# Seven-product pairs at every fourth expert instead of every sixth, with the low parts of their rows made by accumulating transfers

## The chip, the cores and the metric

One core of one Trainium2 chip. The metric is the device time of one launch in microseconds (us); lower is better.

## The reference, cut to what matters

Two transformer blocks run one after the other on 256 tokens of width 1024. The change touches only the last stage, the mixture of experts at the end of the second block:

```
def chunk_fn(args):
    xt, et, gt = args
    act = jax.nn.gelu(jnp.einsum('td,tkd->tk', xt, u_tab[et])) * gt
    return jnp.einsum('tk,tkd->td', act, v_tab[et])
```

There are 128 x 128 experts. Each token picks 128 of them (8 heads with 16 each). The kernel doesn't gather: it computes a dense product of all experts with all tokens, in which the share of an expert that a token didn't pick is zero. The last product is then out[token, d] = sum over all experts of key[expert, token] times v_tab[expert, d], where key is the gated activation.

## The kernel before, in words

**Blocks of experts.** The kernel calls 128 experts with one first index "expert e". Its keys are the 128 x 256 slice `gates_all[:, e, :]` (128 experts by 256 tokens), and its row is a 128 x 1024 piece of v_tab that SP's queue streams from HBM into one of six slots of `ring` (`chunk_done` of the chunk six places earlier frees the slot). The change is in the stage that goes over e = 0 to 125 and adds into PSUM banks. This stage is the last large one; a short tail for two more experts, the final norm and the store follow it.

**Parts.** Each float32 factor is split into a high part, rounded to the format that TensorE multiplies, and the rest, the low part. A product is then three matmuls: high by high, high by low, low by high. ACT makes the high part of a row (`hi`, L747) and of keys (`key_high`, L1147). The low part is a subtraction, whole minus high. DVE makes it for these rows (`lo`, L1369) and keys (`key_low`, L2030); GpSimd (POOL) does so in earlier stages and is idle in this one. There are three places for high rows and three for keys, used in turn.

**One expert, `second(e)`.** Two halves of the tokens by two halves of the width are four products of 128x128 by 128x512, so twelve matmuls (L2781 to L2783).

**A pair, `seven(e)`.** Two experts e and e+1 together are a product of 2x2 blocks, which would be eight block products. The Winograd form of Strassen's method does it with seven, 21 matmuls instead of 24 (L2853 to L2855), from sums and differences of the blocks. The extra work beside the matmuls: four key sums of 128x128 (`sums_of_keys`, L2051 to L2056), four row sums of 128x512 (`first_sum_of_rows`, `sums_of_rows`, L2073 to L2083), and the high and low parts of all these sums (`key_sums_high` and `row_sums_high` on ACT, `key_sums_low` L2060 and `row_sums_low` L2087 on DVE). Of the row of e only the first half is used as it is (`half_of`), of e+1 the whole row. Pairs start at e = 18 and then at every sixth e, 18 pairs in all; the four experts between two pairs use `second`.

**Order.** Each engine has its own list of instructions, written by hand, and semaphores between them. `chunk_done` counts the chunks that TensorE has finished. Within a pair it is raised after the fourth product (the chunk of e is done) and after the seventh (the chunk of e+1 is done). The place of the row sums is reused as that of their low parts, so DVE may begin the sums for the next pair only when the pair before is finished. The same held for the key sums: they lay where their low parts go.

Of the kernel before, what the change touches and what calls it, by code (L numbers as in the profile page):

```python
# [17 lines left out]
P = 128  # L18
# [30 lines left out]
SEVEN_FROM, SEVEN_TO = 18, NA  # L49
# [28 lines left out]

def _split_plan():
# [5 lines left out]
    for name, n in STAGES:  # L85
        for r in range(n):
# [14 lines left out]
            if who:  # L101
                made["hi"] += (name, r) not in OWN
                made[who] += 1
# [6 lines left out]
            lo.append(made[who] if who else None)  # L110
# [37 lines left out]
def build(nc, x_d, meta_d, pos_d, stream_d, cols_d, w1_d, w2_d, w3_d, zt_d, decay_d, dft_d, idft_d, mask_d, sq_d, keys_d, out_d):  # L148
    with ExitStack() as ctx:
# [50 lines left out]
        keys_split = over("keys_split", "aux", NW * CW + 6 * T, [P, 2, 4, P])  # L200
        sums_lo, sums_hi = over("sums_lo", "arena", 0, [P, 4, 512]), over("sums_hi", "arena", 4 * 512, [P, 4, 512])
# [113 lines left out]
        def vt(n):  # L315
# [26 lines left out]
        key_sums = aux[:, NW * CW + 6 * T + 4 * P:NW * CW + 6 * T + 8 * P].rearrange("p (a t) -> p a t", a=4)  # L342
        row_sums = arena[:, 0:4 * 512].rearrange("p (a d) -> p a d", a=4)
# [13 lines left out]
        lo_pool, lo_dve, own_hi = sem("lo_pool"), sem("lo_dve"), sem("own_hi")  # L357
# [18 lines left out]
        loaded_part = [sem(f"loaded_part{n}") for n in range(KT // 2)]  # L376
        flt_pe, flt_arg, flt_sin, flt_k = sem("flt_pe"), sem("flt_arg"), sem("flt_sin"), sem("flt_k")
# [15 lines left out]
        vt_turned, vt_ready, spec_ready, ys_ready = sem("vt_turned"), sem("vt_ready"), sem("spec_ready"), sem("ys_ready")  # L393
# [6 lines left out]
        cv_ready, ce_ready, ew_ready, ew_turned, halves_added = (  # L400
            sem("cv_ready"), sem("ce_ready"), sem("ew_ready"), sem("ew_turned"), sem("halves_added"))
# [3 lines left out]
        xt_turned, xt_ready, xt_added = sem("xt_turned"), sem("xt_ready"), sem("xt_added")  # L405
# [84 lines left out]
        N_SEVEN = (SEVEN_TO - SEVEN_FROM) // 6 - 1  # L490

        def row_of(e, i):

            if i is None:
                return gates_all[:, e, :]
            return gates_all[:, bass.ds(i * 6 + e, 1), :].rearrange("p a t -> p (a t)")
# [5 lines left out]
        def sevens(e):  # L502

            return (e - SEVEN_FROM) // 6
# [116 lines left out]
        def _(pool):  # L621
# [48 lines left out]
            for n, c in enumerate(OWN_CHUNKS):  # L670
# [3 lines left out]
                nc.gpsimd.tensor_copy(hi_part(c), ring[:, c % NS, :]).then_inc(own_hi, 1)  # L674
                if BY[c] == "pool":
                    pool.wait_ge(own_hi, n + 1)
# [17 lines left out]
            lo(base + NA)  # L694
            lo(base + expert_u(NA))
# [3 lines left out]
        def _(act_e):  # L699
# [444 lines left out]
            def key_high(e, i=None, w=T):  # L1144

                act_e.wait_ge(chunk_done, turns(base + NA + e - 2, i, 6))
                A(peer_part[0][:, e % 3, 0:w], row_of(e, i)[:, 0:w], ACT.Copy).then_inc(key_hi, 1)  # L1147

            def key_and_row(e, i=None):

                key_high(e, i)
                hi(base + expert_v(e), 0 if i is None else i, 6 if i is not None else 0)

            def half_of(e, i=None):
# [3 lines left out]
                act_e.wait_ge(landed[c % NS], turns(16 * (c // NS + 1), i, 16))  # L1158
                act_e.wait_ge(chunk_done, turns(BEFORE[c] + 1, i, 6))
                A(hi_part(c)[:, 0:512], ring[:, c % NS, 0:512], ACT.Copy).then_inc(hi_ready, 1)  # L1160

            def key_sums_high(e, i=None):

                act_e.wait_ge(sums_made, turns(8 * sevens(e) + 4, i, 8))
                A(keys_split[:, 0, :, :], key_sums, ACT.Copy).then_inc(sums_hi_ready, 1)

            def row_sums_high(e, half, i=None):

                act_e.wait_ge(sums_made, turns(8 * sevens(e) + 6 + 2 * half, i, 8))
# [8 lines left out]

            for e in range(NW, SEVEN_FROM):
                hi(base + expert_v(e))  # L1180
            key_sums_high(SEVEN_FROM)
            seven_ahead(SEVEN_FROM)
            with act_e.Fori(0, N_SEVEN) as i:
                for m in range(2, 6):
                    key_and_row(SEVEN_FROM + m, i)
                key_sums_high(SEVEN_FROM + 6, i)
                seven_ahead(SEVEN_FROM + 6, i)
            for e in range(SEVEN_TO - 4, NA):
                key_and_row(e)
                if e in (SEVEN_TO - 2, SEVEN_TO - 1):  # L1190
# [1871 lines left out]
```

## Time and profile before

| what | value |
|---|---|
| median of 3 runs | 1702.54 us (1701.95 to 1702.57) |
| the profiled execution | 1702.42 us, of which the trace's span is 1700.6 us |
| TensorE busy | 1684.0 us (99%) |
| VectorE (DVE) busy | 1315.4 us (77%) |
| ScalarE (ACT) busy | 1010.1 us (59%) |
| GpSimd (POOL) busy | 817.2 us (48%), nothing between about 1341 and 1675 us |
| data moved | 296.38 MB, mean 174 GB/s |

The profiled time is 1.8 us longer than the span: start and end lie outside the trace. Matmuls overlap in the trace (each is shown some 390 ns long, though they follow each other more closely), so a busy TensorE doesn't tell how fast it goes; the distance between two starts does. The stage of the change fills most of the time between 1370 and 1680 us.

### The profile page before, as it was taken

What the parts mean: (1) busy time and instruction counts of PE and PEld (TensorE: products, weight loads), DVE (VectorE), ACT (ScalarE), POOL (GpSimd) and SP (SyncE); (2) the same over time, 40 slices, a digit from 0 to 9 for tenths busy, and PEclk for the clock granted to TensorE, in tenths of its full rate; (3) what the DMA queues carried; (4) which work ended last, traced back from release to release, by engine and by line L of the source; (5) the groups of instructions that cost most, each with busy time, mean ns of one, the idle gap of its engine ahead of it and who ended that gap; (6) DMA issues with size and microseconds to landing.
All of it is one profiled execution on the core that took longest, in us unless ns stands there. A gap on an engine that the chain in (4) does not pass through costs nothing.

```text
span 1700.6 us, 33402 instructions
## 1 busy us (share of the span) xinstructions
PE 1684.0 (99%) x11335; PEld 1528.8 (90%) x11335; DVE 1315.4 (77%) x2539; ACT 1010.1 (59%) x1701; POOL 817.2 (48%) x341
## 2 busy tenths in 40 slices
PE   9999999999999999999999999999999999999998
PEld 8988898889998888988999999999999988888887
DVE  6767786566547777869877998777888779999997
ACT  5444632566564445657555555887878546666665
POOL 4666596842766666742006782777777400000001
PEclk9999999999999999999999999999999999999999
DMA  7655454622445554443555455444444555555553
GB/s 252 210 185 190 160 188 148 211 100 100 149 160 187 185 188 171 161 160 127 173 186 186 171 186 178 172 163 162 164 168 165 173 194 194 198 201 193 199 199 116
DMA packets 85841, 296.38 MB, mean 174 GB/s; under 512 B 10548, under 2 KB 14613, under 8 KB 85606
## 3 DMA queue, kind: packets, MB, share of 16 engines
q1 hardware_dynamic: 82480, 290.69, 49.9%
q10 hardware_dynamic: 3254, 4.23, 0.8%
q8 instruction: 72, 1.18, 0.3%
q14 instruction: 35, 0.29, 0.1%
HBM read 293.83 MB, written 1.05 MB: 173 GB/s over the span
## 4 chain that ended last, share of the span: by engine, by line
PE 92%; DVE 5%; ACT 1%; DMA 0%; issue 0%; SPq 0%; POOL 0%; DVEq 0%; POOLq 0%; ACTq 0%
PE ps L2223 15%; PE ps L2225 15%; PE ps L2224 14%; PE ps L2329 6%; PE ps L2781 5%; PE ps L2782 5%; PE ps L2783 5%; PE ps L2330 3%; PE ps L2356 2%; PE ps L2357 2%; PE ps L2478 2%; PE ps L2358 2%; PE ps L2825 2%; PE ps L2853 2%; PE ps L2854 2%; PE ps L2855 2%
## 5 line engine op out<-in xcount | busy, mean ns | idle before, releaser
L2225 PE MATMUL ps<-h_lo_hi,ring_lo 128*128 128x256 f32 (+1 forms) x1888 | 531.5, 282 | 0.0
L627 POOL TENSOR_TENSOR ring_lo<-ring,peer_split 128x1024 fp32r<-128x1024 f32 x117 | 283.7, 2425 | 451.2 <-ACT peer_split L747 448.7
L627 POOL TENSOR_TENSOR ring_lo<-ring,main_hi 128x1024 fp32r<-128x1024 f32 x114 | 285.5, 2505 | 182.6 <-ACT main_hi L747 161.2
L2225 PEld LDWEIGHTS ps<-h_lo_hi,ring_lo 128*128 128x128 f32 x1888 | 355.8, 188 | 0.0
L627 POOL TENSOR_TENSOR ring_lo<-ring,more_hi 128x1024 fp32r<-128x1024 f32 x89 | 229.0, 2573 | 188.6 <-ACT more_hi L747 182.9
L2223 PE MATMUL ps<-h_lo_hi,peer_split 128*128 128x256 f32 x1024 | 288.1, 281 | 0.1
L2224 PE MATMUL ps<-h_lo_hi,peer_split 128*128 128x256 f32 x1024 | 286.8, 280 | 0.0
L747 ACT ACTIVATE peer_split<-ring 128x1024 fp32r<-128x1024 f32 x238 | 249.4, 1048 | 29.4 <-PE ps L2783 29.4
L747 ACT ACTIVATE main_hi<-ring 128x1024 fp32r<-128x1024 f32 x156 | 164.3, 1057 | 96.6 <-DMA ring<-in_stream 72.8
L2224 PEld LDWEIGHTS ps<-h_lo_hi,peer_split 128*128 128x128 f32 x1024 | 193.8, 189 | 0.0
L2223 PEld LDWEIGHTS ps<-h_lo_hi,peer_split 128*128 128x128 f32 x1024 | 193.2, 189 | 0.3 <-issue 0.2
L1369 DVE TENSOR_TENSOR ring_lo<-ring,peer_split 128x1024 fp32r<-128x1024 f32 x121 | 148.8, 1230 | 38.6 <-ACT peer_split L747 38.3
L747 ACT ACTIVATE more_hi<-ring 128x1024 fp32r<-128x1024 f32 x111 | 117.6, 1061 | 92.4 <-DMA ring<-in_stream 82.0
L2223 PE MATMUL ps<-h_lo_hi,main_hi 128*128 128x256 f32 (+1 forms) x504 | 145.1, 288 | 1.5 <-DVE ring_lo L1369 1.1
L2781 PE MATMUL ps<-peer_split 128*128 128x512 f32 x368 | 146.0, 397 | 0.0
L2782 PE MATMUL ps<-ring_lo,peer_split 128*128 128x512 f32 x368 | 144.5, 393 | 0.0
L2783 PE MATMUL ps<-peer_split 128*128 128x512 f32 x368 | 143.6, 390 | 0.0
L2224 PE MATMUL ps<-h_lo_hi,main_hi 128*128 128x256 f32 (+1 forms) x504 | 141.8, 281 | 0.0
L2330 PE MATMUL ps<-h_lo_hi,ring_lo 128*128 128x256 f32 x448 | 125.3, 280 | 0.0
L1147 ACT ACTIVATE peer_split<-arena 128x256 fp32r (+3 forms) x108 | 43.0, 398 | 106.4 <-PE ps L2783 75.4
L2223 PEld LDWEIGHTS ps<-h_lo_hi,main_hi 128*128 128x128 f32 x504 | 95.2, 189 | 8.5 <-issue 6.1
L2224 PEld LDWEIGHTS ps<-h_lo_hi,main_hi 128*128 128x128 f32 x504 | 95.2, 189 | 0.5 <-issue 0.2
(552 smaller groups left out, 4299.9 us busy)
## 6 DMA issues: line engine op xcount, KB each, us to landing
ring<-in_stream SPq DMA_DIRECT2D x550, 512.0 KB, 3.2
x<-in_x SPq DMA_DIRECT2D x4, 256.0 KB, 5.1
arena<-in_decay ACTq DMA_DIRECT2D x4, 256.0 KB
arena<-in_keys ACTq DMA_DIRECT2D x1, 1024.0 KB, 5.5
out<-h SPq DMA_DIRECT2D x7, 128.0 KB, 2.0
arena<-in_mask ACTq DMA_DIRECT2D x1, 768.0 KB, 5.4
aux<-in_dft ACTq DMA_DIRECT2D x4, 72.0 KB
arena<-in_filter_w ACTq DMA_DIRECT2D x1, 260.0 KB
```

The source lines that it names most:

```text
L627: nc.gpsimd.tensor_tensor(ring_lo[:, c % NS, :], ring[:, c % NS, :], hi_part(c).bitcast(F32), ALU.subtract).then_inc(lo_pool, 1)
L747: A(hi_part(c), ring[:, c % NS, :], ACT.Copy).then_inc(hi_ready, 1)
L1147: A(peer_part[0][:, e % 3, 0:w], row_of(e, i)[:, 0:w], ACT.Copy).then_inc(key_hi, 1)
L1369: V.tensor_tensor(ring_lo[:, c % NS, :], ring[:, c % NS, :], hi_part(c).bitcast(F32), ALU.subtract).then_inc(lo_dve, 1)
L2223: M(out, w_hi, parts[0], start=start, stop=False, skip_group_check=True)
L2224: M(out, w_hi, parts[1], start=False, stop=False, skip_group_check=True)
L2225: return M(out, w_lo, parts[0], start=False, stop=stop, skip_group_check=True)
L2329: M(out, hi_part(c)[:, cols_at], h_lo_hi[:, :, k, NM:L], start=(k == 0), stop=False, skip_group_check=True)
L2330: ins = M(out[:, 1, :], ring_lo[:, c % NS, cols_at], h_lo_hi[:, 1, k, NM:L], start=False, stop=(k == KT - 1), skip_group_check=True)
L2781: M(by_token(t, b), a_hi, w_hi, start=begin, stop=False)
L2782: M(by_token(t, b), a_hi, w_lo, start=False, stop=False)
L2783: return M(by_token(t, b), a_lo, w_hi, start=False, stop=end)
```

## The change

From e = 30 on a pair starts at every fourth e, so that two experts by `second` follow each pair. The pairs at 18 and 24 stay as they were, and the ones at 30, 34, ... 122 are new in form: 24 pairs in place of the 16 that stood at 30, 36, ... 120. In these the low parts of the two rows no longer come from DVE. ACT writes the negated high part of the row into a new place `pair_low` (`minus_high`: 128x512 of the row of e, 128x1024 of the row of e+1), and a DMA issued by GpSimd adds the whole row onto it, which leaves whole minus high. TensorE waits for these transfers by two new semaphores, `low_moved[0]` and `low_moved[1]`. ACT still makes the high parts as before. `pair_low` exists once, so ACT may write it only when the chunk of the first expert of the pair before is done. The key sums of these pairs lie in a place of their own (`late_key_sums`), so that DVE can make them while TensorE still uses the parts of the pair before; their high part waits on ACT for the end of that pair. Both new places lie on keys that are used up by then. The loops go over twelve experts at a time instead of six. Three semaphores of earlier stages are merged into one, `side_turned`.

```
 def minus_high(e, i=None):
+    for n, (c, at, width) in enumerate(((base + expert_v(e), 0, 512), (base + expert_v(e + 1), 512, CW))):
+        if n == 0:
+            act_e.wait_ge(chunk_done, turns(base + expert_v(e - 4) + 1, i, GROUP))
+        act_e.wait_ge(landed[c % NS], turns(16 * (c // NS + 1), i, 16 * GROUP // NS))
+        A(pair_low[:, at:at + width], ring[:, c % NS, 0:width], ACT.Copy, scale=-1.0).then_inc(other_hi, 1)
...
 # ACT, for each pair
+def four_behind(e, i=None):
+    key_and_row(e + 2, i)
+    key_and_row(e + 3, i)
+    minus_high(e + 4, i)
+    key_sums_high(e + 4, i)
+    seven_ahead(e + 4, i)
...
 # GpSimd
+for e in range(FOUR_FROM, NA, 4):
+    for n, (c, at, width) in enumerate(((base + expert_v(e), 0, 512), (base + expert_v(e + 1), 512, CW))):
+        pool.wait_ge(other_hi, len(OWN) + 2 * (sevens(e) - 2) + n + 1)
+        pool.dma_start(pair_low[:, at:at + width].bitcast(F32), ring[:, c % NS, 0:width], accum_op=ALU.add).then_inc(low_moved[n], 16)
...
 # DVE, for each pair
+def four_behind(e, i=None):
+    row_sums_low(e, 1, i)
+    row_and_key(e + 2, i)
+    sums_of_keys(e + 4, i)
+    row_and_key(e + 3, i)
+    pair_ahead(e + 4, i)
+
+def pair_ahead(e, i=None):
+    dve.wait_ge(chunk_done, turns(base + expert_v(e - 2), i, GROUP))
     first_sum_of_rows(e, i)
-    half_of(e, i)
     sums_of_rows(e, i)
     key_low(e + 1, i)
+    key_sums_low(e, i)
     dve.wait_ge(sums_made, made(8, e, i))
-    lo(base + expert_v(e + 1), 0 if i is None else i, 6 if i is not None else 0, 6 if i is not None else 0)
     row_sums_low(e, 0, i)
...
 # TensorE
+def both_parts(n, c):
+    if by_dma(e):
+        pe.wait_ge(hi_ready, turns(HI[c], i, GROUP))
+        pe.wait_ge(low_moved[n], turns(16 * (sevens(e) - 1), i, 16 * GROUP // 4))
+    else:
+        low(c)
...
+with pe.Fori(0, N_GROUPS) as i:
+    for m in range(0, GROUP, 4):
+        seven(FOUR_FROM + m, i=i)
+        second(FOUR_FROM + m + 2, i=i, step=GROUP, los=GROUP // 2)
+        second(FOUR_FROM + m + 3, i=i, step=GROUP, los=GROUP // 2)
```

On ACT the loop over the experts stood like this at the step from the single experts to the next pair (L1147 copies keys, L747 a whole row, L1165 the key sums, L1160 half of a row):

```order
L1147 ACTIVATE peer_split<-arena 128x256
L747 ACTIVATE peer_split<-ring 128x1024 [waits chunk_done,landed5]
L1164 ISA
L1165 ACTIVATE keys_split<-aux 128x512 [waits sums_made]
L1146 REGISTER_ALU
L1147 ISA [waits chunk_done]
L1147 ACTIVATE peer_split<-arena 128x128
L1158 REGISTER_ALU
L1160 ACTIVATE peer_split<-ring 128x512 [waits chunk_done,landed0]
```

The same place of the changed kernel (L1167 copies keys, L767 a whole row, L1207 the negated rows, L1187 the key sums, L1180 half of a row):

```order
L1167 ACTIVATE peer_split<-arena 128x256
L767 ACTIVATE peer_split<-ring 128x1024 [waits chunk_done,landed3]
L1207 ACTIVATE pair_low<-ring 128x512 [waits landed4,chunk_done]
L1207 ACTIVATE pair_low<-ring 128x1024 [waits landed5]
L1185 REGISTER_ALU
L1186 ISA [waits chunk_done]
L1187 ACTIVATE keys_split<-arena 128x512 [waits sums_made]
L1163 ISA [waits chunk_done]
L1167 ACTIVATE peer_split<-arena 128x128
L1180 ACTIVATE peer_split<-ring 128x512 [waits chunk_done,landed4]
```

Two copies have come between the last single row and the key sums, and the key sums wait for `chunk_done` too.

On GpSimd nothing stood between the last rows of the stage before and the end of the program:

```order
L626 REGISTER_ALU [waits lo_pool]
L627 TENSOR_TENSOR ring_lo<-ring,peer_split 128x1024 [waits hi_ready]
L632 REGISTER_ALU
L632 COMPARE_AND_BRANCH
L627 TENSOR_TENSOR ring_lo<-ring,peer_split 128x1024 [waits hi_ready,lo_pool] x3
L149 UNCONDITIONAL_BRANCH
```

In the changed kernel 24 times two transfers stand there, of which the first and the last two are shown:

```order
L643 TENSOR_TENSOR ring_lo<-ring,peer_split 128x1024 [waits hi_ready,lo_pool]
L714 DMA pair_low<-ring 128x512 [waits other_hi]
L714 DMA pair_low<-ring 128x1024 [waits other_hi]
...
L714 DMA pair_low<-ring 128x512 [waits other_hi]
L714 DMA pair_low<-ring 128x1024 [waits other_hi]
L643 TENSOR_TENSOR ring_lo<-ring,peer_split 128x1024 [waits hi_ready,lo_pool] x2
L158 UNCONDITIONAL_BRANCH
```

Each transfer waits for one copy of ACT, and nothing else of GpSimd stands between them.

On DVE the work ahead of a pair held two low parts of rows (L2041 and L1369) among the sums of rows (L2080 to L2083) and the keys (L2030):

```order
L2041 TENSOR_TENSOR ring_lo<-ring,peer_split 128x512 [waits sums_made,hi_ready]
L2080 TENSOR_TENSOR arena<-ring,arena 128x512 [waits sums_made,landed1]
L2081 TENSOR_TENSOR arena<-ring 128x512
L2082 REGISTER_ALU
L2083 TENSOR_TENSOR arena<-ring,arena 128x512 [waits sums_made]
L2029 REGISTER_ALU
L2030 TENSOR_TENSOR peer_split<-arena,peer_split 128x256 [waits key_hi]
L2095 REGISTER_ALU
L1368 REGISTER_ALU
L1369 TENSOR_TENSOR ring_lo<-ring,peer_split 128x1024 [waits hi_ready]
```

In the changed kernel they are gone, and the low part of the key sums (L2107) comes after the sums of rows (L2127 to L2132) instead of ahead of them:

```order
L2127 TENSOR_TENSOR arena<-ring,arena 128x512 [waits sums_made]
L2073 REGISTER_ALU
L2074 TENSOR_TENSOR peer_split<-arena,peer_split 128x128 [waits key_hi]
L2130 TENSOR_TENSOR arena<-ring 128x512
L2131 REGISTER_ALU
L2132 TENSOR_TENSOR arena<-ring,arena 128x512 [waits sums_made]
L2073 REGISTER_ALU
L2074 TENSOR_TENSOR peer_split<-arena,peer_split 128x256 [waits key_hi]
L2106 REGISTER_ALU
L2107 TENSOR_TENSOR keys_split<-arena,keys_split 128x512 [waits sums_hi_ready]
```

What stays is one subtraction for keys between the sums of rows, and DVE reads no row's high part for a pair any more.

## Rows read from the trace of the kernel before

**Rows 1.** The page: busy time of each engine, and the chain that ended last.
```profile
PE 1684.0 (99%) x11335; PEld 1528.8 (90%) x11335; DVE 1315.4 (77%) x2539; ACT 1010.1 (59%) x1701; POOL 817.2 (48%) x341
...
PE 92%; DVE 5%; ACT 1%; DMA 0%; issue 0%; SPq 0%; POOL 0%; DVEq 0%; POOLq 0%; ACTq 0%
```

**Rows 2.** Busy time by stretch, 1420 to 1500 us (columns in the first line).
```profile
core 0: us, PE busy (x) PEld busy (x) DVE busy (x) ACT busy (x) POOL busy (x), PEclk, DMA share, GB/s
1420.00:1500.00 80.00, 80.00 (x348) 64.97 (x348) 73.41 (x116) 50.23 (x76) 0.00 (x0) 1.00 0.57 197
```

**Rows 3.** Waits from 1360 to 1690 us: engine, line, waited for, total, times, longest.
```profile
POOL ring_lo L627 <- ACT peer_split L747: 335.0, 2, 334.6
ACT peer_split L1147 <- PE ps L2783: 75.4, 54, 1.9
DVE ring_lo L1369 <- ACT peer_split L747: 32.7, 65, 5.9
ACT peer_split L1147 <- PE ps L2855: 31.0, 36, 1.1
```

**Rows 4.** TensorE's timeline (start, duration): a pair's first, twelfth and last matmul, the next pair.
```profile
1504.56 0.40 PE L2853 MATMUL ps<-peer_split 128*128 128x512 f32 x1
...
1507.11 0.39 PE L2855 MATMUL ps<-sums_hi,keys_split 128*128 128x512 f32 x1
...
1509.18 0.39 PE L2855 MATMUL ps<-sums_hi,peer_split 128*128 128x512 f32 x1
...
1520.50 0.40 PE L2853 MATMUL ps<-peer_split 128*128 128x512 f32 x1
```

**Rows 5.** DVE's timeline around the same pair (start, duration).
```profile
1499.42 0.69 DVE L2060 TENSOR_TENSOR keys_split<-aux,keys_split 128x512 fp32r<-128x512 f32 x1
1500.02 0.69 DVE L2073 TENSOR_TENSOR arena<-ring 128x512 f32<-128x512 f32 x1
1500.63 0.29 DVE L2030 TENSOR_TENSOR peer_split<-arena,peer_split 128x128 fp32r<-128x128 f32 x1
1500.83 0.69 DVE L2041 TENSOR_TENSOR ring_lo<-ring,peer_split 128x512 fp32r<-128x512 f32 x1
...
1506.98 1.23 DVE L1369 TENSOR_TENSOR ring_lo<-ring,peer_split 128x1024 fp32r<-128x1024 f32 x1
1508.11 0.42 DVE L2030 TENSOR_TENSOR peer_split<-arena,peer_split 128x256 fp32r<-128x256 f32 x1
...
1512.24 0.42 DVE L2030 TENSOR_TENSOR peer_split<-arena,peer_split 128x256 fp32r<-128x256 f32 x1
1512.58 0.29 DVE L2051 TENSOR_TENSOR aux<-arena 128x128 f32 x1
...
1512.99 0.28 DVE L2054 TENSOR_TENSOR aux<-aux,arena 128x128 f32<-128x128 f32 x1
1513.40 0.29 DVE L2056 TENSOR_TENSOR aux<-arena,aux 128x128 f32<-128x128 f32 x1
```

**Rows 6.** ACT's timeline around the same pair (start, duration).
```profile
1503.36 2.00 ACT L1170 ACTIVATE sums_hi<-arena 128x1024 fp32r<-128x1024 f32 x2
...
1507.64 0.42 ACT L1147 ACTIVATE peer_split<-arena 128x256 fp32r x1 [1.02 <-PE ps L2855]
1507.96 1.04 ACT L747 ACTIVATE peer_split<-ring 128x1024 fp32r<-128x1024 f32 x1
...
1513.75 0.61 ACT L1165 ACTIVATE keys_split<-aux 128x512 fp32r<-128x512 f32 x1
1515.25 0.31 ACT L1147 ACTIVATE peer_split<-arena 128x128 fp32r x1 [0.89 <-PE ps L2783]
1515.46 0.62 ACT L1160 ACTIVATE peer_split<-ring 128x512 fp32r<-128x512 f32 x1
```

**Rows 7.** DMA from 1500 to 1532 us: packets, MB, share; issues, KB each, us to landing.
```profile
q1 hardware_dynamic: 1728, 6.29, 57.0%
...
ring<-in_stream SPq DMA_DIRECT2D x12, 512.0 KB, 3.2
```

More of the change, by code:

```diff
@@ L76, with by_dma @@
 OUT1_SLOT = (1, 2, 0, 4, 5, 0, 1, 2)
+def by_dma(e):
+    return e >= FOUR_FROM and (e - FOUR_FROM) % 4 < 2
 def _split_plan():
@@ L100, in _split_plan @@
                 who = "dve"
-            if who:
+            if name == "experts" and NA <= r < 2 * NA and by_dma(r - NA):
+                who = "dma"
+                made["hi"] += 1
+            elif who:
                 made["hi"] += (name, r) not in OWN
@@ L109, in _split_plan @@
             hi.append(made["hi"])
-            lo.append(made[who] if who else None)
+            lo.append(made[who] if who in made else None)
             same = [b for b in range(c) if by[b] and slot[b] == slot[c] and (b >= START["experts"]) == (name == "experts")]
@@ L502, in sevens, with sums_of_pair @@
         def sevens(e):
-            return (e - SEVEN_FROM) // 6
+            return (e - SEVEN_FROM) // 6 if e < FOUR_FROM else 2 + (e - FOUR_FROM) // 4
+        def sums_of_pair(e):
+            return late_key_sums if by_dma(e) else key_sums
         LEAD, AFTER = 3, 2
@@ L1151, in key_and_row @@
                 key_high(e, i)
-                hi(base + expert_v(e), 0 if i is None else i, 6 if i is not None else 0)
+                hi(base + expert_v(e), 0 if i is None else i, GROUP if i is not None else 0)
             def half_of(e, i=None):
@@ L2048, in sums_of_keys @@
                 a11, a21, a12, a22 = a0[:, 0:P], a0[:, P:T], a1[:, 0:P], a1[:, P:T]
[L2049 to L2050 removed]
+                s1, s2, s3, s4 = (sums_of_pair(e)[:, n, :] for n in range(4))
+                if by_dma(e):
+                    dve.wait_ge(sums_lo_ready, turns(3 * sevens(e) - 2, i, 9))
+                else:
+                    dve.wait_ge(chunk_done, base + expert_v(e - 4))
                 V.tensor_tensor(s1, a21, a22, ALU.add).then_inc(sums_made, 1)
@@ L2109, in _ @@
             seven_ahead(SEVEN_FROM)
-            with dve.Fori(0, N_SEVEN) as i:
-                row_sums_low(SEVEN_FROM, 1, i)
+            for e in range(SEVEN_FROM, FOUR_FROM, 6):
+                row_sums_low(e, 1)
                 for m in range(2, 5):
-                    row_and_key(SEVEN_FROM + m, i)
-                sums_of_keys(SEVEN_FROM + 6, i)
-                row_and_key(SEVEN_FROM + 5, i)
-                seven_ahead(SEVEN_FROM + 6, i)
-            row_sums_low(SEVEN_TO - 6, 1)
-            for e in range(SEVEN_TO - 4, NA):
-                row_and_key(e)
+                    row_and_key(e + m)
+                sums_of_keys(e + 6)
+                row_and_key(e + 5)
+                if e + 6 < FOUR_FROM:
+                    seven_ahead(e + 6)
+            pair_ahead(FOUR_FROM)
+            with dve.Fori(0, N_GROUPS) as i:
+                for m in range(0, GROUP, 4):
+                    four_behind(FOUR_FROM + m, i)
+            for e in range(FOUR_FROM + N_GROUPS * GROUP, NA - 4, 4):
+                four_behind(e)
+            row_sums_low(NA - 4, 1)
+            row_and_key(NA - 2)
+            row_and_key(NA - 1)
             def expert(tile, n, buf, part):
@@ L2877, in _ @@
                     second(m, i=i, step=6)
-            seven(SEVEN_FROM, begin=True)
-            for m in range(2, 6):
-                second(SEVEN_FROM + m)
-            with pe.Fori(0, N_SEVEN - 1) as i:
-                seven(SEVEN_FROM + 6, i=i)
-                for m in range(8, 12):
-                    second(SEVEN_FROM + m, i=i, step=6)
-            seven(SEVEN_TO - 6, end=True)
-            for e in range(SEVEN_TO - 4, NA):
-                second(e)
+            for e in range(SEVEN_FROM, FOUR_FROM, 6):
+                seven(e, begin=e == SEVEN_FROM)
+                for m in range(2, 6):
+                    second(e + m)
+            with pe.Fori(0, N_GROUPS) as i:
+                for m in range(0, GROUP, 4):
+                    seven(FOUR_FROM + m, i=i)
+                    second(FOUR_FROM + m + 2, i=i, step=GROUP, los=GROUP // 2)
+                    second(FOUR_FROM + m + 3, i=i, step=GROUP, los=GROUP // 2)
+            for e in range(FOUR_FROM + N_GROUPS * GROUP, NA, 4):
+                seven(e, end=e == NA - 4)
+                second(e + 2)
+                second(e + 3)
             pe.wait_ge(sums_kept, 4)
```

137 lines of the change are left out of this document (80 added, 57 removed).

## The prediction

> **What bounds the kernel now.** I read the page's busy times and its chain first [rows 1]: TensorE is busy 99% of the span and holds 92% of the chain that ended last. So a change pays only by giving TensorE less to do, or by ending a wait of TensorE. Next the stage of the change, by stretches [rows 2]: TensorE is busy for all of it at the full granted clock (1.00, which is 2.4 GHz), DVE 73.41 of 80 us, ACT 50.23, POOL not at all, and the DMA engines 0.57 of the time. Then the list of waits there [rows 3]: ACT waits for TensorE, DVE for ACT, and no row says that a matmul waited for anything. POOL's 335.0 us are its pause. TensorE is thus the bound, and its time is the number of matmuls by their spacing.
>
> **The spacing.** A pair starts at 1504.56 and the next at 1520.50 [rows 4]: 15.94 us for 21 + 4 x 12 = 69 matmuls, 0.231 us each, with no gap in between. (The 0.39 to 0.40 us shown for one is its way through a pipeline.)
>
> **What the change removes on TensorE.** From e = 30 there are 24 pairs in place of 16, so 8 more, each with 21 matmuls in place of 24: 24 matmuls by 0.231 are 5.54 us. A group of four experts then takes 21 + 24 = 45 matmuls, 10.40 us. That is all there is to gain, and it holds only while every other engine is done with a group within 10.40 us and every operand is there in time. So I cost each engine per group, counting from start to start in the timeline, since successive instructions of an engine overlap a little.
>
> **DVE, per group.** Four 128x1024 subtractions (two single rows, two halves of the row sums) at 1.13 (1506.98 to 1508.11): 4.52. Five 128x512 ones (four row sums, the key sums' low part) at 0.60 (1499.42 to 1500.02): 3.00. Three key parts at 0.34 (1512.24 to 1512.58): 1.02, and half a key part 0.20 (1500.63 to 1500.83). The four key sums: 1512.58 to the last start at 1513.40 is 0.82, and 0.20 for that one: 1.02. One row sum now needs the one just before it; a dependent start is shown 0.13 after the end of its source (1512.99 + 0.28 to 1513.40), so 0.69 + 0.13 in place of 0.60: 0.22. Sum 9.98 of 10.40 us [rows 5]. The two row parts taken off DVE are 0.60 + 1.13 = 1.73 per pair; with them it would be 11.71, over the limit. So without the transfers the denser pairs could not pay. DVE keeps 0.42 us per group.
>
> **ACT, per group** [rows 6]. Three key copies at 0.32, half of one 0.21, three whole rows at about 0.98, two sums 1.90 together (shown as 2.00), half a row and the key sums some 0.55 each: about 7.1. Added are the negated rows, 128x512 and 128x1024 like the copies there: 0.6 + 1.0. About 8.7 of 10.40: it fits. What matters is where they stand in ACT's list. Queued behind them are the key sums, the half row, the row of e+1 and the row sums of the coming pair, and DVE waits for those. I followed this chain from the start of a pair (0): its twelfth matmul starts 2.55 later, and ACT's key copy 0.53 after that (1507.11 to 1507.64), at 3.1; the row to 4.4; the negated parts end at 5.0 and 5.95; the pair before is over by then (its 21st matmul at 4.6, and 0.5), so the key sums don't wait; half a row to 7.3. The row of e+1 of the coming pair needs the third place of high rows, free after 33 matmuls, 7.6 + 0.5: ACT copies keys and row until 9.5 and row sums to 10.4 and 11.4. DVE finishes the low parts at 11.6 and 12.7. TensorE wants the first with the tenth matmul of the coming pair, 10.40 + 2.08 = 12.5, the second with the sixteenth, 13.9. Spare: 0.9 us at the tightest. I cost these moves at nothing; the cover is this 0.9 us and DVE's 0.42 us.
>
> **The transfers.** POOL has nothing else to do, so it issues each when ACT's copy is done: the 256 KB one at 5.0, the 512 KB one at 5.95. TensorE wants the first at 10.40 and the second three matmuls later, at 11.09. So they may take 5.4 and 5.1 us from issue to landing, and beyond that TensorE stands still in every one of the 23 groups that follow a group of the new form. The trace holds no accumulating transfer, so I bound it. The nearest row is a load of 512 KB: 3.2 us to landing, and twelve of them fill 0.57 of 32 us, so one keeps the 16 engines busy for 1.52 us, and 1.68 us are neither [rows 7]. Floor: 3.2. Two ring loads fall in the same time: the one that replaces the pair's second row (issued at about 5.4) and the one after the next single row (8.1). With an accumulating transfer at the price of a plain one, and all of the 1.68 ahead of the data, data move from 6.7: 0.76 + 1.52, and 1.52 for the first load, end at 10.5; the second load starts to move at 9.8 and shares for 0.7, so 10.5 to 10.9, just inside 11.09. At twice the price (the place is read as well as the source) and with all of both loads ahead of it, 1.52 + 3.04 + 3.04 from 6.7 end at 14.3, 3.2 too late: ceiling 23 x 3.2 = 74 us. I take the plain price, as the nearest row has it, because the 1.68 is not all ahead of the data and the ring load need not win every turn. It is the weakest step of the sum: a delay of 0.24 us per pair eats the whole gain (23 x 0.24 = 5.5).
>
> No row shows what an accumulating transfer costs. The Trainium skill has a rule against it, in *Collectives: The Full Stack*, section "Part 3: Why 7× under link rate — side-by-side accounting": a sum made in the DMA path emits two reads for each write, and such a transfer runs at about half the rate of a copy. By that rule the sum would be that of the first rival below at twice the price, a loss; no run here shows yet whether it holds between two places of SBUF.
>
> **Everything else.** The loads of the ring come as often per matmul as before; the one that must land first, the row of e+1, is issued as a pair starts (0.5), lands at 3.7 and is negated from 5.0 on, 1.3 spare. The unrolled loops and merged semaphores put no work on TensorE. The tail keeps its instructions.
>
> **Sum.** 1702.42 (profiled) less 5.54 is 1696.9; the median of the runs is 0.12 above the profiled one, so 1697.0.
>
> **Rivals.**
> - *The accumulating transfers land late* (the other side). Place: TensorE before the first or fourth matmul of a pair. For it: the window is only 0.2 to 0.6 us wider than a plain price with both ring loads, and an addition must read its place. Against: POOL is free and the DMA engines idle for 0.43 of the time. It decides from a landing of 5.3 us on. At one and a half times the plain price, data end at 6.7 + 1.14 + 2.28 + 1.52 = 11.6 and 12.1 with the second load: 1.05 late, 24 us, so 1721. At twice: 12.8, some 13.6 with the load, 2.5 late, 57 us, so 1754; if half of the 1.68 lies behind or is not there, some 1730. Chance 0.31.
> - *DVE becomes the bound.* It would fill 96% of a group, where it fills 92% now. If each of its 14 instructions cost 0.05 more, 9.98 becomes 10.68, 0.28 over: 23 x 0.28 = 6.4, so 1703. Against it: the prices come from the same instructions in the same stage. Chance 0.09.
> - *Ring loads land late*, because the added 768 KB per pair sit before them. If the row of e+1 is negated 0.6 us later for it, the second transfer lands 0.5 us late: 11.5 less 5.5, so 1708. Chance 0.05.
> - *The change doesn't do what it says*: the matmuls go, but TensorE's time is taken back a little everywhere, 1700 to 1704. Chance 0.03.
>
> **How the numbers follow.** The forecast, no wait of TensorE, has 0.52. Its own range is 1695.8 to 1699.0. A measurement of this kernel can tell about 0.2%, 3.4 us, from no change. Faster by more than that: 0.52. Within it: 0.03 of the late transfers (0.09 to 0.39 us per pair), 0.05 of DVE, 0.01 of the loads and 0.03 of the last rival, 0.12. Slower: the remaining 0.36. The range has to reach into the late transfers: up to 1735 it leaves out some 0.11 above and 0.03 below 1695.8.
>
> **What would show it.** Right: no wait of a matmul on `low_moved`, 45 matmuls in 10.40 us, transfers that land within 5.1 us, DVE at about 0.96. Wrong: a gap before each pair's first or fourth matmul, with the row that follows it released by a DMA; then the price of the accumulating transfers failed. A gap before the tenth or sixteenth would say that ACT's longer list failed, and a gap before a single expert that DVE did.

## The result, and the profile after

The changed kernel took 1804.66 us in the median (1802.60 to 1809.15, 4 runs), beside 1702.24 us for the kernel before on the same chip. The ratio is 1.0605, with a 95% interval of 1.0592 to 1.0618: 102 us slower, where 5.5 us faster was forecast and the range ended at 1735.

The page of the changed kernel, the lines that answer to [rows 1]:

```profile
PE 1722.0 (95%) x11311; PEld 1546.0 (86%) x11311; DVE 1313.8 (73%) x2579; ACT 1056.9 (58%) x1773; POOL 859.4 (48%) x389
...
PE 79%; DMA 9%; DVE 5%; ACT 3%; issue 2%; POOL 1%; SPq 0%; ACTq 0%; DVEq 0%; POOLq 0%
```

TensorE has the 24 matmuls less (11311 for 11335), but is busy longer, and 9% of the chain that ended last are now a DMA. A busy time that grows while the count falls says that something got slower, not only later. The same stretch as [rows 2]:

```profile
1420.00:1500.00 80.00, 64.95 (x235) 49.52 (x234) 51.74 (x90) 43.80 (x67) 8.60 (x10) 0.87 0.69 186
```

235 matmuls instead of 348 in 80 us. TensorE stood still for 15 us of them, DVE fell from 73.41 to 51.74 (so it isn't the bound), and the granted clock is 0.87 of full speed. The waits of the stage, as in [rows 3], below POOL's own pause (316.0 us):

```profile
ACT peer_split L1167 <- PE ps L2937: 99.6, 22, 6.9
DVE ring_lo L1413 <- ACT peer_split L767: 79.6, 34, 5.6
PE ps L2935 <- DMA pair_low<-ring: 46.3, 23, 3.4
PEld ps L2935 <- issue: 34.4, 21, 3.9
PEld ps L2935 <- DVE peer_split L2074: 28.9, 9, 3.6
```

The longest of these rows are followers: DVE waits for ACT, and ACT for TensorE. TensorE waits at one line, L2935, the first matmul of a block product of a pair. PE and PEld (its weight loads) wait at the same time, so their rows must not be added. The row that names DVE is the same wait with another name: TensorE waits there for several things, and a kernel that differs only in the transfer (below, `e1_no_transfer`) has no such row. One pair, to be held against [rows 4]:

```profile
1485.62 0.49 PE L2935 MATMUL ps<-peer_split 128*128 128x512 f32 x1
1485.95 0.40 PE L2936 MATMUL ps<-pair_low,peer_split 128*128 128x512 f32 x1
1486.19 0.40 PE L2937 MATMUL ps<-peer_split 128*128 128x512 f32 x1
1489.33 0.79 PE L2935 MATMUL ps<-peer_split 128*128 128x512 f32 x1 [2.74 <-DMA pair_low<-ring]
1489.91 0.63 PE L2936 MATMUL ps<-pair_low,peer_split 128*128 128x512 f32 x1
1490.34 0.63 PE L2937 MATMUL ps<-peer_split 128*128 128x512 f32 x1
...
1495.04 0.52 PE L2936 MATMUL ps<-sums_lo,keys_split 128*128 128x512 f32 x1
1495.39 0.39 PE L2937 MATMUL ps<-sums_hi,keys_split 128*128 128x512 f32 x1
1495.62 0.40 PE L2935 MATMUL ps<-sums_hi,peer_split 128*128 128x512 f32 x1
...
1501.87 0.40 PE L2935 MATMUL ps<-peer_split 128*128 128x512 f32 x1
```

Three things are to be seen. The fourth matmul, the first that needs the second transfer, stands 2.9 us late (1486.19 to 1489.33, where 0.23 is due). After it, matmuls follow each other at 0.43 us in place of 0.23: TensorE had stood still, and its clock fell to the lower of its two levels (1.2 GHz in place of 2.4) until 1495, which the granted clock of 0.50 in this stretch shows:

```profile
1489.40:1495.00 5.60, 5.60 (x13) 4.38 (x14) 0.54 (x3) 1.33 (x3) 0.00 (x0) 0.50 0.13 37
```

14 steps took 6.06 us where 3.23 were due, another 2.8 us. And the group takes 16.25 us to the next pair, where 10.40 were forecast. The chain of the same pair tells where the transfer's time went:

```profile
1478.95 0.53 ACT pair_low L1207
1479.77 0.86 POOL pair_low L714
1480.72 8.38 DMA pair_low<-ring
1489.33 0.79 PE ps L2935
```

From GpSimd's first issue (1479.77) to the second landing (1489.10) are 9.33 us. DMA from 1478 to 1490 us, as in [rows 7]:

```profile
q1 hardware_dynamic: 573, 2.09, 54.1%
q0 software_dynamic: 288, 0.79, 34.1%
issues: line engine op xcount, KB each, median us to landing
ring<-in_stream SPq DMA_DIRECT2D x3, 512.0 KB, 4.9
pair_low<-ring POOLq DMA_DIRECT2D x1, 512.0 KB, 8.4
pair_low<-ring POOLq DMA_DIRECT2D x1, 256.0 KB, 5.7
```

The pair's 0.79 MB took 34.1% of 12 us, 4.1 us of all 16 engines; the ring's 2.09 MB, 2.6 times as many bytes, took 6.5 us. A byte of an accumulating transfer kept the engines busy 1.7 times as long as one from HBM in this stretch. Within the 9.33 us alone, 1479.77 to 1489.10, the ring's queue (q1) and GpSimd's (q0) filled the engines almost wholly:

```profile
q1 hardware_dynamic: 408, 1.47, 50.2%
q0 software_dynamic: 288, 0.79, 43.9%
```

So the ring's loads took 4.7 us of it, for 1.47 MB or nearly three loads, the pair's own transfers 4.1, and about 0.5 us were neither.

Over all 23 groups, from the starts of the matmuls in the trace: the first pair of the new form starts at 1424.82 and the 24th at 1770.58, 15.03 us per group. The mean of the gap ahead of a pair's first matmul is 0.37 us, ahead of the fourth 2.76, and the steps after it are 1.46 us longer than at full clock, in 16 of the 23 groups by 1.5 us or more and in 7 by 0.1. 23 x (0.37 + 2.76) are 72 us of waiting and 23 x 1.46 are 34 us of the lower clock; less the 5.5 us saved that makes 100 of the 106.7 us by which this span (1807.3 us; the execution shown is the slowest of the four) is longer than the one before (1700.6). In three of the 7 groups without the lower clock the wait ahead of the fourth matmul was 1.8 us or less; in the other four it was 2.7 to 3.2, as long as in the 16.

### The profile page after: what moved, and what is told of

Its sections match the earlier page's. It is cut to its first block, busy times and chain, and to the rows that moved or that the text cites. A ratio compares the mean times of both kernels' runs of the same rounds, so it can differ in the third digit from the quotient of the medians.

```text
span 1807.3 us, 33438 instructions
## 1 busy us (share of the span) xinstructions
PE 1722.0 (95%) x11311; PEld 1546.0 (86%) x11311; DVE 1313.8 (73%) x2579; ACT 1056.9 (58%) x1773; POOL 859.4 (48%) x389
## 4 chain that ended last, share of the span: by engine, by line
PE 79%; DMA 9%; DVE 5%; ACT 3%; issue 2%; POOL 1%; SPq 0%; ACTq 0%; DVEq 0%; POOLq 0%
PE ps L2295 14%; PE ps L2297 14%; PE ps L2296 13%; DMA pair_low<-ring 8%; PE ps L2401 6%; PE ps L2402 3%; PE ps L2935 2%; PE ps L2428 2%; PE ps L2429 2%; PE ps L2550 2%; PE ps L2430 2%; PE ps L2936 2%; PE ps L2937 2%; PE ps L2897 2%; PE ps L2853 2%
## 5 line engine op out<-in xcount | busy, mean ns | idle before, releaser
L767 ACT ACTIVATE peer_split<-ring 128x1024 fp32r<-128x1024 f32 x230 | 240.9, 1048 | 27.1 <-PE ps L2855 27.1
L714 POOL DMA_DIRECT2D pair_low<-ring x48 | 41.5, 865 | 384.5 <-ACT pair_low L1207 382.4
L767 ACT ACTIVATE main_hi<-ring 128x1024 fp32r<-128x1024 f32 x156 | 164.5, 1057 | 95.4 <-DMA ring<-in_stream 70.6
L1413 DVE TENSOR_TENSOR ring_lo<-ring,peer_split 128x1024 fp32r<-128x1024 f32 x89 | 110.7, 1244 | 117.3 <-ACT peer_split L767 117.0
L767 ACT ACTIVATE more_hi<-ring 128x1024 fp32r<-128x1024 f32 x111 | 117.5, 1061 | 85.2 <-DMA ring<-in_stream 79.2
L1167 ACT ACTIVATE peer_split<-arena 128x256 fp32r (+3 forms) x108 | 41.5, 384 | 167.3 <-PE ps L2937 134.1
L2853 PE MATMUL ps<-peer_split 128*128 128x512 f32 x304 | 120.5, 396 | 0.6 <-DVE peer_split L2200 0.6
L2854 PE MATMUL ps<-ring_lo,peer_split 128*128 128x512 f32 x304 | 119.4, 393 | 0.0
L2855 PE MATMUL ps<-peer_split 128*128 128x512 f32 x304 | 118.8, 391 | 0.0
L2295 PEld LDWEIGHTS ps<-h_lo_hi,main_hi 128*128 128x128 f32 x504 | 95.2, 189 | 8.5 <-issue 6.1
```

The lines of the kernel that those rows point to most:

```text
L714: pool.dma_start(pair_low[:, at:at + width].bitcast(F32), ring[:, c % NS, 0:width], accum_op=ALU.add).then_inc(low_moved[n], 16)
L767: A(hi_part(c), ring[:, c % NS, :], ACT.Copy).then_inc(hi_ready, 1)
L1413: V.tensor_tensor(ring_lo[:, c % NS, :], ring[:, c % NS, :], hi_part(c).bitcast(F32), ALU.subtract).then_inc(lo_dve, 1)
L2295: M(out, w_hi, parts[0], start=start, stop=False, skip_group_check=True)
L2853: M(by_token(t, b), a_hi, w_hi, start=begin, stop=False)
L2854: M(by_token(t, b), a_hi, w_lo, start=False, stop=False)
```

## The experiments

All change the new kernel, and all times are medians beside the kernel before on the same chip (1702.5 to 1702.8 us; the runs come from several chips, so a few tenths of a us between two of them mean nothing).

### e1_no_transfer: the change without its transfers

GpSimd issues nothing, and TensorE waits for ACT's negated copies where it waited for the transfers; the low parts of the pairs' rows are then the negated high parts.

```
-    pe.wait_ge(low_moved[n], turns(16 * (sevens(e) - 1), i, 16 * GROUP // 4))
+    pe.wait_ge(other_hi, turns(len(OWN) + 2 * (sevens(e) - 2) + n + 1, i, 2 * GROUP // 4))
```

> The accumulating transfers are left out, and TensorE waits for ACT's negated copies in their place; the low parts of the pairs' rows are then wrong (negated high parts). Everything else of the change stays. Theory (the transfers alone are late, the rest of the change fits as summed): no gap before a pair's matmuls, 10.40 us per group of four, about 1697 us. Rival (the longer lists of ACT and DVE are themselves too slow): groups of over 10.6 us with gaps before the tenth matmul or before single experts, 1703 us or more.

Measured 1696.55 us (ratio 0.9964, 0.9950 to 0.9979), 0.5 us from the forecast of 1697.0. The stretch from 1500 us:

```profile
1500.00:1580.00 80.00, 80.00 (x350) 65.29 (x349) 76.25 (x135) 66.04 (x102) 0.00 (x0) 1.00 0.61 203
```

TensorE never waits, at the full clock, and DVE is at 0.953: 9.86 us of a group of 10.35 (its pairs start at 1425.84 and, 23 groups later, at 1663.81). So the count of matmuls, DVE's sum and ACT's longer list were right, and all 108 us between the two kernels belong to the transfers.

### e2_plain_copy: the same transfers without the addition

```
-pool.dma_start(pair_low[...], ring[:, c % NS, 0:width], accum_op=ALU.add)
+pool.dma_start(pair_low[...], ring[:, c % NS, 0:width])
```

> The same transfers from GpSimd's queue, as plain copies: the row replaces the negated high part, so the low parts are wrong. Theory (the addition makes a transfer twice as dear, since its place is read too): the engine time per pair falls from 4.3 us to about 2.2, the 512 KB transfer lands some 2 to 3 us sooner than 8.2 us, in 5.5 to 6, which leaves 0.5 to 1 us of wait per pair: 1705 to 1725 us. Rival (the fixed part of a transfer from GpSimd's queue is what is late, 0.86 us of issue and some 2.5 us until data move): landing stays at 7 us or more, 1760 us or more.

Measured 1722.49 us (1.0113, 1.0096 to 1.0130). DMA from 1500 to 1580 us:

```profile
q1 hardware_dynamic: 4049, 14.74, 58.4%
q0 software_dynamic: 1568, 5.51, 17.1%
...
ring<-in_stream SPq DMA_DIRECT2D x28, 512.0 KB, 4.2
pair_low<-ring POOLq DMA_DIRECT2D x7, 512.0 KB, 5.5
pair_low<-ring POOLq DMA_DIRECT2D x7, 256.0 KB, 5.1
```

A plain copy takes 17.1% of 80 us for 5.51 MB, 2.5 us per MB. The accumulating one in the same stretch of the changed kernel took 30.5% for 4.46 MB, 5.5 us per MB: 2.2 times as much. But the plain price doesn't fit either. 5.5 us are more than the window of 5.1, pairs wait 0.39 + 0.67 us in the mean, and 23 x 1.06 = 24 us undo the forecast four times over.

### e3_traffic_only: the traffic without the wait

The same accumulating transfers run onto `pair_low` from a place of keys, and TensorE neither waits for them nor reads them (it takes the high part in place of the low one); ACT waits for a transfer before it writes the place again.

```
-pool.dma_start(pair_low[...], ring[:, c % NS, 0:width], accum_op=ALU.add)
+pool.dma_start(pair_low[...], arena[:, 124 * T:124 * T + width], accum_op=ALU.add)
...
-    pe.wait_ge(low_moved[n], turns(16 * (sevens(e) - 1), i, 16 * GROUP // 4))
...
-    return hi_part(c)[:, at], pair_low[:, 0:512] if c == c0 else pair_low[:, 512:512 + CW][:, at]
+    return hi_part(c)[:, at], hi_part(c)[:, at]
```

> The transfers run with the same sizes and additions, but from a source that nobody overwrites, and TensorE neither waits for them nor reads what they make (it uses the high parts twice, so the result is wrong); only the next negated copy waits for them. Theory (TensorE's wait for the landing is the cost): close to the kernel without transfers, 1697 to 1705 us. Rival (the traffic itself is the cost, because the loads of the ring come late): gaps stay, before other matmuls, 1740 us or more.

Measured 1702.64 us (1.000, 0.9990 to 1.0009): 6.1 us above the kernel without transfers. From 1500 to 1580 us:

```profile
1500.00:1580.00 80.00, 79.17 (x340) 62.79 (x339) 74.50 (x129) 63.80 (x96) 12.74 (x15) 1.00 0.99 272
```

The ring's loads in the same stretch:

```profile
ring<-in_stream SPq DMA_DIRECT2D x30, 512.0 KB, 6.3
```

With no wait for them, 768 KB per group fill the DMA engines to 0.99 and ring loads take 6.3 us instead of 3.2, and yet this costs only the gain (groups of 10.60 us in place of 10.35). The other 102 us come with TensorE's wait for the landing.

### e4_busy_waits: zeros multiplied during the wait

TensorE does two matmuls of zeros ahead of a pair's first and eleven ahead of its fourth, into a bank that they leave unchanged (GpSimd writes the zeros once, ahead of the pairs).

```
+def stay_busy(n):
+    if by_dma(e):
+        for _ in range(n):
+            M(ps[:, 7, :], fill[:, 0:P], fill[:, :], start=False, stop=False)
+
+stay_busy(2)
 both_parts(0, c0)
...
+stay_busy(11)
 both_parts(1, c1)
```

> As the changed kernel, but TensorE multiplies zeros (2 matmuls ahead of a pair's first wait, 11 ahead of the second, 3.0 us per pair in all), which add nothing to the result, and so is idle for less of the waits. Theory (part of the loss is the granted clock, which falls from 1.00 after a wait and costs 1.5 us of slow matmuls per pair): the slow matmuls go, 24 x 1.5 us are saved, 1765 to 1775 us. Rival (the slow matmuls have another cause, such as the reads of the transfers beside them): no gain, 1800 us or more.

Measured 1790.43 us (1.0513, 1.0495 to 1.0530), 14.2 us less than the changed kernel: outside both ranges, and less than the 34 us that the lower clock costs by the trace. One pair:

```profile
1485.08 2.67 PE L2945 MATMUL ps<-fill 128*128 128x512 f32 x11
1488.23 0.49 PE L2938 MATMUL ps<-peer_split 128*128 128x512 f32 x1 [0.48 <-DMA pair_low<-ring]
1488.56 0.39 PE L2939 MATMUL ps<-pair_low,peer_split 128*128 128x512 f32 x1
1488.79 0.40 PE L2940 MATMUL ps<-peer_split 128*128 128x512 f32 x1
```

The steps after the wait are 0.23 us again, in all 23 groups (0.09 us over in place of 1.46), and the granted clock is 1.00. But the gaps, zeros included, are longer, 0.81 and 2.95 us in place of 0.37 and 2.76: the two matmuls ahead of the first are done even where its transfer has landed. So 23 x 1.37 = 31.5 us of slow steps went and 23 x 0.63 = 14.5 us of gaps came, which leaves 17, the difference of the two traces (1807.3 and 1790.2 us). The transfers still ran beside the matmuls, so the fall of the clock follows from standing still and not from their traffic; the net gain is 14 us by the medians.

### e5_half_bytes: half the columns

```
-pool.dma_start(pair_low[:, at:at + width]..., ring[:, c % NS, 0:width], accum_op=ALU.add)
+pool.dma_start(pair_low[:, at:at + width // 2]..., ring[:, c % NS, 0:width // 2], accum_op=ALU.add)
```

> The accumulating transfers cover only the first half of their columns (128x256 and 128x512 in place of 128x512 and 128x1024), so the low parts of the other columns stay the negated high parts. Theory (the price goes by bytes, an accumulating byte costs two plain ones): the transfers then load the DMA engines like the plain copies of full size, which took 1722.5 us, so 1712 to 1730 us, the second landing 5 to 6 us after its issue in place of 8.2, and little or no slow spacing of matmuls. Rival (an accumulating transfer has a long fixed part, whatever its bytes): landing stays at 7 us or more, waits of 2 us or more per pair, 1765 us or more.

Measured 1723.65 us (1.0119, 1.0102 to 1.0135), 1.2 us from the plain copies of twice the bytes. From 1500 to 1580 us:

```profile
q0 software_dynamic: 2016, 2.75, 21.0%
...
pair_low<-ring POOLq DMA_DIRECT2D x7, 256.0 KB, 5.6
pair_low<-ring POOLq DMA_DIRECT2D x7, 128.0 KB, 5.2
```

The second landing is 5.6 us in place of 8.0, so a long fixed part isn't the cause; the first stays at 5.2 with half its bytes, so bytes aren't all of it either. In time an added byte came out like two copied ones. On the DMA engines it cost 6.1 us per MB here (21.0% of 80 us for 2.75 MB), 2.4 times the plain copy's, and 2.2 times at full columns. The Trainium skill has two reads for each write and half the rate of a copy for the sums of a collective, in *Collectives: The Full Stack*, section "Part 3: Why 7× under link rate — side-by-side accounting"; these traces agree, with 2.2 and 2.4 times between two places of SBUF.

### e6_act_queue: plain copies from ACT's queue

GpSimd issues nothing; ACT issues the copies of `e2_plain_copy` itself, behind its two negated rows.

```
+    act_e.wait_ge(other_hi, ...)
+    nc.scalar.dma_start(pair_low[...], ring[:, c % NS, 0:width]).then_inc(low_moved[n], 16)
```

> Plain copies in place of accumulating ones (so the low parts are the whole rows), issued from ACT's queue instead of GpSimd's. Theory (part of the lateness of the plain copies, 1722.5 us, is GpSimd's queue: its instruction of some 0.54 us and the time until its first packet moves): landings drop to about 4 us, below the windows of 5.4 and 5.1 us, and the time to 1696 to 1704 us. Rival (the queue is alike, the sharing with the ring loads makes the lateness): landing stays at 5 us or more, 1715 to 1725 us.

Measured 1709.01 us (1.0030, 1.0019 to 1.0042), between both ranges. From 1500 to 1580 us:

```profile
pair_low<-ring ACTq DMA_DIRECT2D x8, 512.0 KB, 5.0
pair_low<-ring ACTq DMA_DIRECT2D x7, 256.0 KB, 3.2
```

The 256 KB land in 3.2 us where GpSimd's take 5.1, so 13.5 us of the plain copies' loss go with GpSimd's queue. The packets tell where: the first of a pair moved 1.0 to 1.2 us after ACT's issue and 2.8 to 3.0 us after GpSimd's (in each of six pairs of either trace). The 512 KB still take 5.0 beside the ring loads. For the additions it is no way out by the Trainium skill, which ties accumulation to GpSimd (*DMA: Bandwidth & Descriptors*, section "SWDGE vs HWDGE vs iDMA"); no run here tries it from another queue.

### e7_dve_lows: denser pairs with DVE making the low parts

```
 # ACT, four_behind
-    minus_high(e + 4, i)
...
 # DVE, pair_ahead
+    V.tensor_tensor(ring_lo[:, c % NS, 0:512], ring[:, c % NS, 0:512], hi_part(c)[:, 0:512].bitcast(F32), ALU.subtract).then_inc(lo_dve, 1)
...
+    lo(base + expert_v(e + 1), 0 if i is None else i, GROUP if i is not None else 0)
...
 # TensorE, both_parts
-    pe.wait_ge(low_moved[n], turns(16 * (sevens(e) - 1), i, 16 * GROUP // 4))
+    low(c, 0 if i is None else i, 0 if i is None else GROUP)
```

> The denser pairs without any transfer: DVE subtracts the low parts of the pairs' rows, as in the pairs before the change. By the prediction's sum DVE then needs 9.98 + 1.73 = 11.71 us per group of 10.40, so 23 x 1.3 = 30 us are lost against 1696.6: 1722 to 1732 us, with DVE busy all the time and waits of matmuls on DVE. Rival (DVE's sum is too high, and the transfers were never needed): 1697 to 1703 us. A fall of the granted clock would show as matmuls 0.43 apart and would add to either.

Measured 1727.63 us (1.0144, 1.0127 to 1.0161). The stretch from 1500 us:

```profile
1500.00:1580.00 80.00, 72.92 (x310) 57.25 (x309) 78.81 (x133) 50.49 (x77) 0.00 (x0) 1.00 0.54 183
```

The wait of TensorE from 1420 to 1690 us:

```profile
PE ps L2924 <- DVE ring_lo L1404: 22.2, 22, 1.1
```

DVE is at 0.985 and sets the pace: pairs start at 1483.77 and, 17 groups later, at 1681.94, 11.66 us each against 11.71 by the prediction's sum. TensorE waits some 1.2 us per group here, mostly in one piece, and keeps its full clock.

### e8_early: negated 1.3 us earlier

```
 key_and_row(e + 2, i)
-key_and_row(e + 3, i)
 minus_high(e + 4, i)
+key_and_row(e + 3, i)
 key_sums_high(e + 4, i)
```

> ACT writes the negated rows before the key copy and row of the last single expert, 1.3 us earlier, all else as in the changed kernel. Theory (the landing is what TensorE waits for, 2.76 us before the fourth matmul and 0.37 before the first): the windows are 1.3 us wider, so each pair waits 1.3 us less, 23 x 1.3 = 30 us, and the slow spacing after shorter waits is less too: 1745 to 1778 us. Rival (the DMA engines are full, or the ring loads move along, so the transfers land no earlier): 1790 us or more.

Measured 1775.37 us (1.0424, 1.0402 to 1.0446), within the theory's range, but not by its mechanism. From 1500 to 1580 us:

```profile
ring<-in_stream SPq DMA_DIRECT2D x24, 512.0 KB, 5.6
pair_low<-ring POOLq DMA_DIRECT2D x6, 512.0 KB, 9.0
pair_low<-ring POOLq DMA_DIRECT2D x6, 256.0 KB, 5.7
```

The second transfer now lands after 9.0 us, beside ring loads that take 5.6, and the gap ahead of the fourth matmul is 2.78 us as before (2.76). What fell is the gap ahead of the first (0.37 to 0.05) and the lower clock (1.46 to 0.48): 23 x 1.3 = 30 us. For the second transfer the rival was right. The lower clock cost about 1.5 us or more at only 4 of the 24 pairs here, though TensorE waits as long ahead of the fourth matmul as before.

### e9_keys_moved: the transfers on operands known early

A version that follows from the runs above. A row streams in just before it is used; the keys lie in SBUF from the start of the stage. DVE gets the rows' low parts back, and the transfers make the keys' low parts, which takes three key parts and a half, 1.22 us per group, off DVE. ACT negates the keys two groups ahead. In DVE's order of row sums no sum follows directly on one that it needs.

```
 # ACT
+def minus_keys(e, i=None):
+    for n in range(2):
...
+        A(key_lows[n][:, at:at + 2, :], keys, ACT.Copy, scale=-1.0).then_inc(other_hi, 1)
...
     key_and_row(e + 3, i)
-    minus_high(e + 4, i)
+    if moved(e + 8):
+        minus_keys(e + 8, i)
...
 # GpSimd
+    pool.dma_start(key_lows[n][:, at:at + 2, :].bitcast(F32), gates_all[:, e + 2 * n:e + 2 * n + 2, :], accum_op=ALU.add).then_inc(low_moved[n], 16)
```

> The same denser pairs, but the rows' low parts are DVE's again, and the accumulating transfers make the low parts of the keys (two transfers of 256 KB per group, for all groups but the last), which ACT negates two groups ahead, since the keys lie in SBUF from the start of the stage. Theory (what the change got wrong is the operand: with a window of more than ten us in place of 5.1, the double price of the transfers costs no wait): DVE sheds 3 x 0.34 + 0.20 = 1.22 of the 11.66 us per group that the denser pairs took without transfers, and two dependent starts of 0.13 by another order of the row sums, so 10.2 of 10.35 us: no matmul waits for a transfer, 1697 to 1700 us, which beats the kernel before. Rival (the traffic alone eats the gain, as 768 KB per group did at 1702.6 us; 512 KB would cost 4 us by that): ring loads land at 4 us or later and TensorE waits for DVE behind them, 1700 to 1704 us. A third way (DVE stays the bound at 10.44 or more): waits of matmuls on DVE with loads as quick as before, 1699 to 1702 us.

Measured 1697.99 us (0.9973, 0.9963 to 0.9984): 4.6 us faster than the kernel before, and the fastest here that makes every low part. From 1500 to 1580 us:

```profile
1500.00:1580.00 80.00, 80.00 (x348) 65.06 (x347) 78.88 (x118) 62.95 (x101) 13.97 (x16) 1.00 0.88 250
```

DMA in the same stretch:

```profile
ring<-in_stream SPq DMA_DIRECT2D x31, 512.0 KB, 4.4
key_lows<-arena POOLq DMA_DIRECT2D x16, 256.0 KB, 6.5
```

The 256 KB land no faster (6.5 us, 5.2 in the changed kernel) and the DMA engines are fuller (0.88, there 0.72), but no matmul waits in this stretch: pairs start at 1424.00 and, 22 groups later, at 1653.25, 10.42 us each. DVE at 0.986 is now level with TensorE.

### e10_short_lead and e11_order_only: what made it fast

The first negates the keys one group ahead in place of two.

```
-    if moved(e + 8):
-        minus_keys(e + 8, i)
+    if moved(e + 4):
+        minus_keys(e + 4, i)
```

> As the kernel whose transfers make the keys' low parts (1698.0 us), but ACT negates the keys one group ahead in place of two: same transfers, same traffic, and a window of about 5.2 us for the first transfer (issued at 1502.61 where the next pair starts at 1507.84) in place of 15.6. Theory (the window decides, and 256 KB take 5.2 to 6.8 us to land): the first transfer is 0 to 1.6 us late for each pair, so a wait of the first matmul of most pairs, and 1703 to 1730 us. Rival (the lead doesn't matter, it was the smaller traffic that made it fast): 1697 to 1700 us.

Measured 1708.18 us (1.0034, 1.0022 to 1.0045), with this row among the waits from 1420 to 1690 us:

```profile
PEld ps L2958 <- DMA key_lows<-arena: 10.3, 17, 1.3
```

The transfers still land in 6.6 us, and 10 us are lost at the same traffic: there the window decides. Against the changed kernel the amount differs too (512 KB per group in place of 768), and no run parts the two. The second has only the new order of DVE's sums, without any transfer:

```
+V.tensor_tensor(t3, b22, b12, ALU.subtract).then_inc(sums_made, 1)
 dve.wait_ge(sums_made, made(5, e, i))
 V.tensor_tensor(t2, b22, t1, ALU.subtract).then_inc(sums_made, 1)
...
-V.tensor_tensor(t3, b22, b12, ALU.subtract).then_inc(sums_made, 1)
-dve.wait_ge(sums_made, made(6, e, i))
+dve.wait_ge(sums_made, made(7, e, i))
 V.tensor_tensor(t4, b21, t2, ALU.subtract).then_inc(sums_made, 1)
```

> The denser pairs without transfers (1727.6 us), with only the other order of DVE's row sums, which the kernel with the moved keys has too. Theory (that kernel is faster because its transfers take 1.22 us of key parts off DVE): the order alone saves one dependent start of 0.12 us per group, 3 us in all, so 1723 to 1728 us. Rival (the order did it): below 1705 us.

Measured 1723.15 us (1.0120, 1.0103 to 1.0137), 4.5 us less than `e7_dve_lows`: the order gives that little, and the other 25 us to `e9_keys_moved` came with moving the key parts (23 x 1.22 = 28 by the prediction's prices).

## Why the prediction was wrong

- **The count of matmuls, DVE's sum, ACT's list: right.** Without the transfers the same lists run at 10.35 us per group (10.40 forecast) and 1696.55 us (1697.0 forecast), DVE at 9.86 us (9.98). That DVE couldn't keep the pairs' low parts was right too, 11.66 us for 11.71.
- **The step that failed: "I take the plain price, as the nearest row has it".** The bounds were drawn rightly and the wrong end was taken. The ceiling had 9.3 us from the first issue to the second landing (5.0 to 14.3) and 3.2 us of delay; the pair above took 9.33, and the mean delay is 0.37 + 2.76 = 3.13. The text named the second read of an addition as the reason for the ceiling, and then went by the row of a load, which has no such read.
- **The plain price was itself too low, in the landing and not on the engines.** A plain copy kept the engines busy no longer than the load of the row (2.5 us per MB; 1.52 us for 512 KB are 2.9). But plain copies from GpSimd land after 5.5 us where 5.1 were to be had, and cost 1722.5 us. The row of a load from SP's queue says nothing of GpSimd's queue, from which the first packet of a plain copy moved 2.8 us or more after the issue where the sum had 1.68: the same 256 KB land 1.9 us earlier from ACT's.
- **"The 1.68 is not all ahead of the data and the ring load need not win every turn" was no reason.** The ring loads slowed too (3.2 to 4.9 us), but the landing came out as if both stood ahead of it. That the ceiling's 9.3 us meet the 9.33 so well is in part luck, since its terms were 1.68 of neither, 3.04 for two ring loads and 4.56 for the pair, and the trace has 0.5, 4.7 and 4.1.
- **A term was missing: the clock.** The rivals priced a wait as its own length. Here the matmuls after it ran at half the rate in 16 of 23 groups, 34 us by the trace; `e4_busy_waits` takes nearly all of them away, and 14 remain as a net gain beside its longer gaps. Without it the time would have been near 1769 us (1696.9 + 72), a little under the ceiling. The rival at twice the price, 1754, had the price nearly right and lacked these 34 us and 15 of waiting (72 for 57).
- **The range** reached only half-way into the late transfers, to 1735, and had no case of the ceiling's 1771 (1697 + 74), though a delay of 0.24 us per pair was known to undo the gain.
- **A smaller slip:** the rival on DVE counts 14 instructions per group, where the prediction's own list has 17 (four and five subtractions, four key parts, four key sums); at 0.05 us more each that is 23 x 0.43 = 10 us over the forecast, 1707. It changed nothing, since DVE took less than forecast.
- **What stays open:** why the clock fell at 16 pairs and not at four with waits as long, nor at most pairs of `e8_early`; and whether the additions would land in time without ring loads beside them, which no run tries.

## What to carry to other kernels

A transfer on the path is priced from its landing, with its own queue, its own reads and every load that runs beside it; when it fits only at the cheapest of these, count it as late. Give to DMA the operand that is known longest, not the one that is largest: the same kind of transfer cost 102 us on rows that had just landed, and on keys that were there from the start, with two thirds of the bytes, no matmul waited for it in the stretch shown. And price a wait of TensorE at more than its length, since the matmuls behind it may run at the lower clock.

## What the runs showed of the hardware

- An accumulating transfer between two places of SBUF takes 2.2 times the DMA engines' time of a plain copy per byte (5.5 and 2.5 us per MB; 2.4 times at half the columns), and GpSimd's instruction for it takes 0.865 us, where the plain copy's takes 0.54:

```profile
L714 POOL DMA_DIRECT2D pair_low<-ring x48 | 41.5, 865 | 384.5 <-ACT pair_low L1207 382.4
```

- From GpSimd's issue of a plain copy to its first packet were 2.8 to 3.0 us, from ACT's 1.0 to 1.2 (six pairs each); of an accumulating one 1.4 to 3.8 (nine pairs of the changed kernel).
- DMA engines at 0.99 for 240 us, with ring loads at 6.3 us in place of 3.2, cost TensorE only 6 us when it waited for none of the added transfers.
- After a wait of 2.7 us matmuls stood 0.43 us apart for 6 us at a granted clock of 0.50, and with zeros multiplied during the wait 0.23. It came after 16 of 23 waits of the changed kernel, and not after all the long ones.
